# A fused hybrid-transformer kernel: query and key projections in another order, value products moved behind the first attention scores, and the meta keys of all heads handled once per query tile

## The chip, the cores and the metric

The kernel runs on one core of a Trainium2 chip. The metric is the device time of one execution in microseconds (us); lower is better.

## What is computed

Two transformer layers follow one another on a sequence of 512 tokens, with 16 meta tokens put in front (528 positions, width 1024). The change touches the first layer's latent attention (8 heads):

```python
q = (rmsnorm(c_q_raw, q_norm) @ w_uq).reshape(b, length, MLA_HEADS, MLA_NOPE + MLA_ROPE)
kv = (rmsnorm(c_kv_raw, kv_norm) @ w_ukv).reshape(b, length, MLA_HEADS, MLA_NOPE + MLA_V)
...
s = (jnp.einsum('bqhd,bkhd->bhqk', qn_b, k_nope)
     + jnp.einsum('bqhd,bkd->bhqk', qr_b, k_rope)).astype(jnp.float32) * scale
...
p = jax.nn.softmax(s, axis=-1).astype(v.dtype)
return jnp.einsum('bhqk,bkhd->bqhd', p, v)
```

The mask is causal. Beside it the first layer has a feed-forward block, a gated delta rule (a recurrence over chunks of 64) and another feed-forward block; the second layer has two more attentions. Everything is float32.

## The kernel before

The program is written out by hand, engine by engine: each engine has its own list of instructions, and counted semaphores order them. Nothing is scheduled by a tool, so the order in the code is the order on the engine, and a wait blocks everything behind it on that engine.

Most matrix products split both operands into a high and a low part (`WHI`, `WLO` of the weights, `CHI`, `CLO` of the latents) and do three fast products for one exact one (`mm3`, lines 562 to 564). Attention itself uses plain float32 products. The scratch memory for results, PSUM, has eight banks of 128 x 512 values; which bank is free decides much of the order. `PS[:, b, ...]` is bank b.

In the stretch that the change touches (about 498 to 604 us of the profiled execution) TensorE does, in order:

- **Queries**: eight tiles `t` of the query projection. Tiles 4 to 7 hold the rotary parts and go to banks 0 to 3, from where VectorE reads them (`ROT`, lines 1921 to 1927). Then it sums squares of the delta rule's queries and keys (`GSQ`, line 690, banks 4 and 5), and does tiles 2, 3, 0 and 1 (banks 6, 7, 4, 5). ScalarE takes logarithms of the sums (line 1333), switches its table to exp (line 1335), and copies the four query tiles (`QH`, line 1340).
- **Keys**: tiles 0, 1, 3, 2, two banks each, copied by ScalarE (`KH`, line 1345).
- **Values**: five tiles in the order meta tokens, then four blocks of 128 tokens (lines 716 to 718), copied by VectorE (`VM`, lines 1934 and 1937).
- **Attention** (`latent_attention`, once on each engine): 16 steps, in `LATENT`. A step is one tile of 128 queries for two heads (p = 0 and 1); the last query tile comes first. Steps 0 to 3 see 528 keys, more than a bank holds, so each head takes two banks and the next step's scores must wait until exp has read them (`WIDE` is 4). Later steps see 400, 272 and 144 keys and alternate between two pairs of banks.

In turn i TensorE does the scores of step i (line 774), transposes the probabilities of step i - 2 (line 785: the blocks of 128 keys; line 792: the 16 meta keys), and multiplies values by the probabilities of step i - 3 (line 808 for the blocks, line 813 for the meta keys). After the last step of a query tile it also spreads the softmax factors (line 824). `per_token` (lines 729 and 732) is a small piece of the delta rule done in turn 1. VectorE takes the row minima (lines 1949 and 1954; scores are negated), ScalarE the exponentials with their sums (`PB`, line 1365). ScalarE copies head 0's transposed blocks (`PTS`, line 1356) and the meta keys' ones of both heads (`PTM`, line 1358); VectorE copies head 1's (line 1968). In turns 6 to 13 VectorE also works on a convolution of the delta rule (`value_taps`, lines 1806 and 1809). GpSimd prepares exponents for the delta rule (lines 534 to 543) that ScalarE needs in turn 13 (`EU`, line 1381) and turn 17 (`IT`, line 1386).

Of the kernel before, what the change touches and what calls it, by code (L numbers as in the profile page):

```python
# [17 lines left out]
P = 128  # L18
# [3 lines left out]
T1 = N_META + SEQ  # L22
# [45 lines left out]
for _name, _c in [("ident", 128), ("ones", 128), ("bones", 128), ("cos", T1), ("sin", T1),  # L68
                  ("mA", 256), ("mB", 256), ("cneg", 4 * NCMP), ("c01", 4 * NCMP), ("i64", CH),
                  ("mlater", CH), ("hs", 4 * NH), ("lvl", LEVELS * CH), ("sel", 4 * 128),  # L70
                  ("oh", 383)]:
    TABS[_name] = _n
    _n += _c
# [4 lines left out]
def build(nc, io):  # L78
# [44 lines left out]
    def region(start, *items):  # L123
# [32 lines left out]
    VM, PB1, PTS1, PTM, DSB1, OTF1, NM1, RS1, RI1, NMF1, a_at1 = region(  # L156
        a_qk, ("VM", [P, 5, SEQ], f32), ("PB1", [P, 2, 2, T1], f32), ("PTS1", [P, 2, 2, SEQ], f32),
        ("PTM", [N_META, 2, 2, P], f32), ("DSB1", [P, SEQ], f32), ("OTF1", [P, SEQ], f32),
        ("NM1", [P, 4 * NH], f32), ("RS1", [P, 4 * NH], f32), ("RI1", [P, 4 * NH], f32),
        ("NMF1", [P, 4 * NH], f32))  # L160

# [109 lines left out]
    def halves(ap):  # L271
# [58 lines left out]
    vm_rdy, fm_rdy, row_st, kx_ld, qx_ld, px_d = (sem(x) for x in (  # L330
        "value_tile_copied", "latent_far_min_ready", "gate_rows_stored", "k_rows_spread",
# [114 lines left out]
    WIDE = sum(x["n"] > SEQ for x in LATENT)  # L446

# [109 lines left out]
    def _(pe):  # L557
# [124 lines left out]
        for t in (4, 5, 6, 7, 2, 3, 0, 1):  # L682
            if t == 2:

                pe.wait_ge(evac, START["uq"])
                pe.wait_ge(l_sq, 8)
                for b, (a, m) in enumerate(spans(0, T1)):
                    for g in range(4):
                        for i in range(2):
                            last = mm(PS[32 + 32 * i:40 + 32 * i, 4 + b, 0:m], tab("hs", NH * g, NH * (g + 1)),  # L690
                                      GSQ[:, 4 * i + g, a:a + m], start=g == 0, stop=g == 3)
                last.then_inc(l_ss, 1)
            elif t == 0:
                pe.wait_ge(l_r, 2)
# [3 lines left out]
            last.then_inc(uq_ps, 1)  # L698
        pe.wait_ge(uq_ps, 8)
        pe.sem_inc(mm_done, 1)  # L700

        pe.wait_ge(lo_rdy, START["ukv"] + 2)
        for t in (0, 1, 3, 2):
            if t == 0:
                pe.wait_ge(rot_rdy, 1)
            elif t >= 2:
                pe.wait_ge(q_act, 4 if t == 3 else 8)
            for b, (a, m) in enumerate(spans(0, T1)):
# [47 lines left out]
        def latent_attention():  # L756
            n = len(LATENT)
            for i in range(n + 3):
                if i < n:
                    x, s = LATENT[i], i % 2  # L760
                    if i == 0:
                        pe.wait_ge(vm_rdy, 4)
                    elif i == WIDE:
# [11 lines left out]
                    last.then_inc(s_ps, 1)  # L775
                if i == 1:
                    per_token()
                if 0 <= i - 2 < n:
                    x, s = LATENT[i - 2], i % 2
                    for p in range(2):  # L780
                        pe.wait_ge(exp_rdy, 2 * (i - 2) + p + 1)
                        if i >= 3:
# [1811 lines left out]
```

## Time and profile before

| | us |
|---|---|
| Median of 3 runs | 1636.67 |
| Lowest and highest run | 1636.23, 1639.49 |
| The profiled execution, its own time | 1633.94 |
| Its span, first to last instruction | 1632.3 |
| TensorE busy | 1574.4 (96%) |
| VectorE busy | 922.6 (57%) |
| ScalarE busy | 577.4 (35%) |
| GpSimd busy | 43.7 (3%) |
| Mean granted TensorE clock | 0.988 of full |

Busy shares are averages over stages with different limits. The granted clock is the share of TensorE's full speed that the chip allowed; it has two levels here, 1.0 (2.4 GHz) and 0.5 (1.2 GHz).

### The profile page before, as it was taken

To read this page: it belongs to the slowest core of one execution; us is meant where nothing else is said; L and a number is where in the kernel's file an instruction comes from. 1 tells how busy PE (TensorE), PEld (TensorE's weight loads), DVE (VectorE), ACT (ScalarE), POOL (GpSimd) and SP (SyncE) were. 2 spreads that over 40 slices of the span, in tenths; PEclk is the share of its full clock that TensorE was granted. 3 is DMA by queue.
4 is the path that set the end of the run, shared out by engine and by line. 5 is a ranking of instruction groups with operands and counts; after the bars stand their busy time and mean duration, and the time that the engine had idled before them with its cause. 6 is when DMAs were issued, how large, how long until landed. Compare 5 with 4: busy or idle time off the path is not lost.

```text
span 1632.3 us, 30415 instructions
## 1 busy us (share of the span) xinstructions
PE 1574.4 (96%) x12739; PEld 1366.1 (84%) x12739; DVE 922.6 (57%) x1408; ACT 577.4 (35%) x854; POOL 43.7 (3%) x41
## 2 busy tenths in 40 slices
PE   6999999999998998989999999999999899999998
PEld 6999999999996678877888888888888687775777
DVE  6655245556487478655444645533555643557872
ACT  5222122223255371224223322222222243556750
POOL 0000000000000600000000000000000000000000
PEclk9999999999999799999999999999999999999999
DMA  6443333332217300001323222232222433120002
GB/s 258 152 144 99 105 128 130 132 98 106 98 60 129 71 2 29 4 3 54 114 81 113 103 98 83 78 114 104 103 87 89 146 148 130 52 68 24 2 2 77
DMA packets 27476, 147.68 MB, mean 90 GB/s; under 512 B 2816, under 2 KB 3088, under 8 KB 16752
## 3 DMA queue, kind: packets, MB, share of 16 engines
q1 hardware_dynamic: 21616, 122.46, 21.7%
q0 software_dynamic: 5232, 22.68, 4.9%
q8 instruction: 78, 1.28, 0.3%
q10 hardware_dynamic: 528, 1.08, 0.2%
q14 instruction: 22, 0.18, 0.0%
HBM read 140.94 MB, written 5.27 MB: 90 GB/s over the span
## 4 chain that ended last, share of the span: by engine, by line
PE 88%; DVE 7%; issue 2%; ACT 2%; DMA 0%; DVEq 0%; SPq 0%; ACTq 0%
PE PS L562 24%; PE PS L563 24%; PE PS L564 24%; PE PS L842 2%; PE PS L852 2%; PE PS L877 2%; PE PS L774 2%; PE PS L864 1%; DVE UMB L2107 1%; DVE TTT L2139 1%; DVE WLO L1623 1%; PE PS L921 1%; PE PS L1147 1%; PE PS L937 1%; PE PS L785 1%
## 5 line engine op out<-in xcount | busy, mean ns | idle before, releaser
L562 PE MATMUL PS<-UH,WHI 128*128 128x264 f32 (+1 forms) x1120 | 337.2, 301 | 14.8 <-DVE UL L1633 11.1
L563 PE MATMUL PS<-UH,WLO 128*128 128x264 f32 (+1 forms) x1120 | 335.6, 300 | 0.0
L564 PE MATMUL PS<-UL,WHI 128*128 128x264 f32 (+1 forms) x1120 | 335.2, 299 | 0.0
L1194 ACT ACTIVATE WHI<-RAW 128x2048 fp32r<-128x2048 f32 (+3 forms) x124 | 210.3, 1696 | 293.6 <-PE PS L564 286.8
L1623 DVE TENSOR_TENSOR WLO<-RAW,WHI 128x2048 fp32r<-128x2048 f32 (+3 forms) x124 | 251.2, 2026 | 80.7 <-ACT WHI L1194 80.1
L562 PEld LDWEIGHTS PS<-UH,WHI 128*128 128x128 f32 x1120 | 211.8, 189 | 21.9 <-DVE WLO L1731 11.1
L563 PEld LDWEIGHTS PS<-UH,WLO 128*128 128x128 f32 x1120 | 211.8, 189 | 6.4 <-issue 0.2
L564 PEld LDWEIGHTS PS<-UL,WHI 128*128 128x128 f32 x1120 | 211.4, 189 | 6.3
L562 PE MATMUL PS<-UHS,WHI 128*128 128x512 f32 x520 | 205.2, 395 | 0.0
L564 PE MATMUL PS<-ULS,WHI 128*128 128x512 f32 x520 | 202.6, 390 | 0.0
L563 PE MATMUL PS<-UHS,WLO 128*128 128x512 f32 x520 | 202.5, 389 | 0.0
L1238 ACT ACTIVATE TANH<-SILU 128x528 f32<-128x528 f32 (+1 forms) x44 | 28.1, 639 | 258.3 <-DVE SILU L1683 258.3
L562 PEld LDWEIGHTS PS<-UHS,WHI 128*128 128x128 f32 x520 | 97.7, 188 | 22.1 <-issue 2.2
L563 PEld LDWEIGHTS PS<-UHS,WLO 128*128 128x128 f32 x520 | 97.7, 188 | 20.9 <-issue 1.0
L564 PEld LDWEIGHTS PS<-ULS,WHI 128*128 128x128 f32 x520 | 97.6, 188 | 20.2
L563 PE MATMUL PS<-GH,WLO 128*128 128x264 f32 x352 | 100.6, 286 | 0.0
L564 PE MATMUL PS<-GL,WHI 128*128 128x264 f32 x352 | 100.3, 285 | 0.0
L562 PE MATMUL PS<-GH,WHI 128*128 128x264 f32 x352 | 99.6, 283 | 0.0
L1683 DVE TENSOR_TENSOR SILU<-PS,RSTD 128x528 f32<-128x528 f32 (+1 forms) x44 | 30.8, 700 | 106.9 <-PE PS L564 104.4
L1708 DVE SCALAR_TENSOR_TENSOR H<-PS,H 128x528 f32<-128x528 f32 (+3 forms) x32 | 22.3, 698 | 112.5 <-PE PS L564 112.5
L562 PE MATMUL PS<-GHS,WHI 128*128 128x512 f32 x176 | 68.7, 390 | 0.0
L563 PE MATMUL PS<-GHS,WLO 128*128 128x512 f32 x176 | 68.5, 389 | 0.0
(403 smaller groups left out, 2703.5 us busy)
## 6 DMA issues: line engine op xcount, KB each, us to landing
RAW<-in_f2u SPq DMA_DIRECT2D x22, 1024.0 KB, 4.8
RAW<-in_f1u SPq DMA_DIRECT2D x21, 1024.0 KB, 4.8
ADA<-in_ada POOLq DMA_DIRECT2D x24, 512.0 KB, 4.5
RAW<-in_f1d SPq DMA_DIRECT2D x16, 704.0 KB, 4.1
RAW<-in_f2d SPq DMA_DIRECT2D x16, 704.0 KB, 4.1
RAW<-in_wi SPq DMA_DIRECT2D x10, 1024.0 KB, 4.8
RAW<-in_w SPq DMA_DIRECT2D x8, 1024.0 KB, 4.8
RAW<-in_mg SPq DMA_DIRECT2D x8, 1024.0 KB, 4.8
```

The source lines that it names most:

```text
L562: mm(out, WHI[:, slot, c:c + w], hi, start=first, stop=False)
L563: mm(out, WLO[:, slot, c:c + w], hi, start=False, stop=False)
L564: return mm(out, WHI[:, slot, c:c + w], lo, start=False, stop=last)
L774: last = mm(scores(i, p, k0, k1), q, KH[0:96, h, k0:k1], start=True, stop=True)
L842: last = mm(PS[:, 2 - 2 * s + p, c:c + m], P2[rows, q, P * x["qi"]:P * (x["qi"] + 1)], P2[rows, 10 + x["b"], a:a + m], start=True, stop=True)
L852: last = nc.tensor.transpose(PS[:, 4 + p, t * P:(t + 1) * P], PB2[:, s, p, t * P:(t + 1) * P], IDENT)
L877: last = mm(PS[rows, 6, P * x["j"]:P * (x["j"] + 1)], v, PTS2[:, s, p, t * P:(t + 1) * P], start=t == 0, stop=t == tiles_ - 1)
L1194: A(WHI[:, slot, 0:w], RAW[:, slot, 0:w], ACT.Copy).then_inc(hi_rdy, 1)
L1238: A(TANH[:, slot, 0:w], SILU[:, slot, 0:w], ACT.Tanh, scale=0.5).then_inc(tanh_rdy, 1)
L1623: TT(WLO[:, slot, 0:w], RAW[:, slot, 0:w], WHI[:, slot, 0:w].bitcast(f32), ALU.subtract).then_inc(lo_rdy, 1)
L1683: TT(SILU[:, slot, 0:w], psum(4 * slot, w), RSTD[:, c0:c0 + w], ALU.mult).then_inc(gn_rdy, 1)
L1708: STT(h, psum(4 * slot, w), 0.25, h, ALU.mult, ALU.add)\
```

## The change

- **Queries**: tiles 2 and 3 come before the sums of squares, tiles 0 and 1 after the keys' tiles 1, 0 and 3.
- **Keys**: tiles 1 and 0 are copied by VectorE, ahead of its `gate_exponents`; tiles 3 and 2 by ScalarE. ScalarE copies query tiles 2 and 3 before the logarithms.
- **Values**: two tiles before the first scores, two behind the scores of step 0, the meta tokens' behind those of step 1. VectorE copies each where its turn allows.
- **Minima**: in the four wide steps each head has its own semaphore count, reduction and minimum, so that head 0's exp does not wait for head 1's scores.
- **Meta keys**: VectorE copies each step's 16 meta probabilities of both heads into `PM` (128 x 2 x 8 heads x 16). Once per query tile TensorE transposes all 128 at once and multiplies them by a value tile in which the meta values stand once for each head, masked (`hm`), four products of full width. Since products of all heads now add to bank 6 over four steps, each query tile begins with a product of zeros that clears the bank. Per step, the two small transposes (line 792), the four records of small products (line 813) and ScalarE's `PTM` copy go.

```diff
+    def scored(i, p):
+
+        return 2 * i + p + 1 if i < WIDE else WIDE + i + 1
...
-        for t in (4, 5, 6, 7, 2, 3, 0, 1):
-            if t == 2:
-
-                pe.wait_ge(evac, START["uq"])
-                pe.wait_ge(l_sq, 8)
...
+        def up_query(t):
+
             for k in range(2):
                 last = mm3(PS[:, (t + 4) % 8, 0:SEQ], 0, (2 * t + k) * P, CHI[:, k, N_META:T1],
                            CLO[:, k, N_META:T1], k == 0, k == 1)
             last.then_inc(uq_ps, 1)
+
+        def up_key(t, b0):
+
+            for b, (a, m) in enumerate(spans(0, T1)):
+                last = mm3(PS[:, b0 + b, 0:m], 1, t * P, CHI[:, 2, a:a + m], CLO[:, 2, a:a + m], True, True)
+            last.then_inc(kn_ps, 1)
+
+        def up_value(t, b):
+
+            out = PS[:, b, 0:SEQ]
+
+            a = N_META + P * (t - 1)
+            hi, lo = (c[:, 2, a:a + P] for c in (CHI, CLO)) if t else (CHM[:, i, :] for i in range(2))
+            mm(out, hi, WHI[:, 1, SEQ:2 * SEQ], start=True, stop=False)
+            mm(out, lo, WHI[:, 1, SEQ:2 * SEQ], start=False, stop=False)
+            mm(out, hi, WLO[:, 1, SEQ:2 * SEQ], start=False, stop=True).then_inc(kn_ps, 1)
+
+        for t in (4, 5, 6, 7):
+            up_query(t)
+        pe.wait_ge(evac, START["uq"])
+        for t in (2, 3):
+            up_query(t)
+        pe.wait_ge(l_sq, 8)
+        for b, (a, m) in enumerate(spans(0, T1)):
+            for g in range(4):
+                for i in range(2):
+                    last = mm(PS[32 + 32 * i:40 + 32 * i, 4 + b, 0:m], tab("hs", NH * g, NH * (g + 1)),
+                              GSQ[:, 4 * i + g, a:a + m], start=g == 0, stop=g == 3)
+        last.then_inc(l_ss, 1)
+        pe.wait_ge(lo_rdy, START["ukv"] + 2)
+        pe.wait_ge(rot_rdy, 1)
+        up_key(1, 2)
+        up_key(0, 0)
+        pe.wait_ge(q_act, 4)
+        up_key(3, 6)
+        pe.wait_ge(l_r, 2)
+        for t in (0, 1):
+            up_query(t)
+        pe.wait_ge(kv_rdy, 2)
+        up_key(2, 2)
         pe.wait_ge(uq_ps, 8)
         pe.sem_inc(mm_done, 1)
-
-        pe.wait_ge(lo_rdy, START["ukv"] + 2)
-        for t in (0, 1, 3, 2):
-            if t == 0:
-                pe.wait_ge(rot_rdy, 1)
-            elif t >= 2:
-                pe.wait_ge(q_act, 4 if t == 3 else 8)
-            for b, (a, m) in enumerate(spans(0, T1)):
-                last = mm3(PS[:, 2 * t + b, 0:m], 1, t * P, CHI[:, 2, a:a + m], CLO[:, 2, a:a + m],
-                           True, True)
-            last.then_inc(kn_ps, 1)
-        for t in range(5):
-            if t % 2 == 0:
-                pe.wait_ge(k_act, t + 2)
-            a = 0 if t == 0 else N_META + P * (t - 1)
-            mm(PS[:, (0, 1, 2, 3, 6)[t], 0:SEQ], CHI[:, 2, a:a + P], WHI[:, 1, SEQ:2 * SEQ], start=True, stop=False)
-            mm(PS[:, (0, 1, 2, 3, 6)[t], 0:SEQ], CLO[:, 2, a:a + P], WHI[:, 1, SEQ:2 * SEQ], start=False, stop=False)
-            mm(PS[:, (0, 1, 2, 3, 6)[t], 0:SEQ], CHI[:, 2, a:a + P], WLO[:, 1, SEQ:2 * SEQ], start=False, stop=True)\
-                .then_inc(kn_ps, 1)
-        pe.wait_ge(kn_ps, 9)
-        pe.sem_inc(mm_done, 1)
+        pe.wait_ge(q_act, 8)
+        for t in (1, 2):
+            up_value(t, 3 + t)
...
+                        if i < WIDE or p:
+                            last.then_inc(s_ps, 1)
+                if i == 0:
+
+                    pe.wait_ge(k_act, 2)
+                    for t in (3, 4):
+                        up_value(t, 3 + t)
                 if i == 1:
+
+                    pe.wait_ge(kv_rdy, 6)
+                    up_value(0, 4)
+                    pe.wait_ge(kv_rdy, 8)
                     per_token()
+                    pe.wait_ge(kn_ps, 9)
+                    pe.sem_inc(mm_done, 1)
...
-                        if p == 0:
-                            last.then_inc(pt_ps, 1)
-                    if x["g"]:
-                        pe.wait_ge(den_rdy, x["g"])
-                    for p in range(2):
-                        last = nc.tensor.transpose(PS[0:N_META, 7, P * p:P * (p + 1)], PB1[:, s, p, 0:N_META], IDENT)
-                    last.then_inc(pt_ps, 1)
+                        last.then_inc(pt_ps, 1)
+                        if p == 0 and x["last"]:
+
+                            pe.wait_ge(pc_rdy1, i - 2)
+                            if x["g"]:
+                                pe.wait_ge(den_rdy, x["g"])
+                            nc.tensor.transpose(PS[:, 7, 0:P], PM[:, x["g"] % 2, :, :].rearrange("q h m -> q (h m)"),
+                                                IDENT)
...
+                    if x["j"] == 0:
+
+                        mm(PS[:, 6, :], ZERO[:, :], ZERO[:, :].unsqueeze(1).to_broadcast([P, 4, P]), start=True,
+                           stop=False)
                     for t in range(x["qi"] + 1):
                         for p in range(2):
                             h = x["j"] + 4 * p
-                            mm(PS[CH * p:CH * (p + 1), 6, P * x["j"]:P * (x["j"] + 1)],
-                               VM[:, 1 + t, CH * h:CH * (h + 1)], PTS1[:, s, p, t * P:(t + 1) * P],
-                               start=t == 0, stop=False)
-                    for p in range(2):
-                        h = x["j"] + 4 * p
-                        last = mm(PS[CH * p:CH * (p + 1), 6, P * x["j"]:P * (x["j"] + 1)],
-                                  VM[0:N_META, 0, CH * h:CH * (h + 1)], PTM[:, s, p, :], start=False, stop=True)
+                            last = mm(PS[CH * p:CH * (p + 1), 6, P * x["j"]:P * (x["j"] + 1)],
+                                      VM[:, 1 + t, CH * h:CH * (h + 1)], PTS1[:, s, p, t * P:(t + 1) * P],
+                                      start=False, stop=False)
+                    if x["last"]:
+                        for j in range(4):
+                            last = mm(PS[:, 6, P * j:P * (j + 1)], VM[:, 0, P * j:P * (j + 1)], PTM[:, :],
+                                      start=False, stop=j == 3)
...
+        def copy_query(i, t):
+
+            act.wait_ge(uq_ps, 4 + i + 1)
+            for p in range(2):
+                A(QH[0:CH, 2 * t + p, :], PS[CH * p:CH * (p + 1), 4 + t, 0:SEQ], ACT.Copy,
+                  scale=scale).then_inc(q_act, 1)
+
+        def copy_key(i, t, b):
+
+            act.wait_ge(kn_ps, i)
+            for p in range(2):
+                A(halves(KH[0:CH, 2 * t + p, :]), PS[CH * p:CH * (p + 1), b:b + 2, 0:HT], ACT.Copy).then_inc(k_act, 1)
+
+        copy_query(0, 2)
+        copy_query(1, 3)
+        chain(A(CST[:, 3:4], EPS_AP, ACT.Ln))
         act.wait_ge(gt_d, 4)
         act.wait_ge(l_ss, 1)
         for i, rows in enumerate((R8, A8)):
             A(RW[R8, i, PAD:].rearrange("p (b n) -> p b n", b=2), PS[rows, 4:6, 0:HT], ACT.Ln,
               bias=CST[rows, 4 + i:5 + i], scale=64.0 if i == 0 else 1.0).then_inc(l_r, 1)
         chain(A(CST[:, 3:4], EPS_AP, ACT.Exp))
-        scale = -float(96) ** -0.5
-        for i, t in enumerate((2, 3, 0, 1)):
-            act.wait_ge(uq_ps, 4 + i + 1)
-            for p in range(2):
-                A(QH[0:CH, 2 * t + p, :], PS[CH * p:CH * (p + 1), 4 + t, 0:SEQ], ACT.Copy,
-                  scale=scale).then_inc(q_act, 1)
-        for i, t in enumerate((0, 1, 3, 2)):
-            act.wait_ge(kn_ps, i + 1)
-            for p in range(2):
-                A(halves(KH[0:CH, 2 * t + p, :]), PS[CH * p:CH * (p + 1), 2 * t:2 * t + 2, 0:HT],
-                  ACT.Copy).then_inc(k_act, 1)
+        copy_key(3, 3, 6)
+        copy_query(2, 0)
+        copy_query(3, 1)
+        copy_key(4, 2, 2)
...
-                    A(PTS1[:, s, 0, 0:w], PS[:, 4, 0:w], ACT.Copy)
+                    last = A(PTS1[:, s, 0, 0:w], PS[:, 4, 0:w], ACT.Copy)
                     act.wait_ge(pt_ps, 2 * (i - 2) + 2)
-                    A(PTM[:, s, :, :], PS[0:N_META, 7, 0:2 * P].rearrange("m (p q) -> m p q", p=2), ACT.Copy)\
-                        .then_inc(pt_rdy, 1)
+                    if LATENT[i - 2]["last"]:
+                        last = A(PTM[:, :], PS[:, 7, 0:P], ACT.Copy)
+                    last.then_inc(pt_rdy, 1)
...
+        for i, t in enumerate((1, 0)):
+            dve.wait_ge(kn_ps, i + 1)
+            for p in range(2):
+                V.tensor_copy(halves(KH[0:CH, 2 * t + p, :]), PS[CH * p:CH * (p + 1), 2 * t:2 * t + 2, 0:HT])\
+                    .then_inc(kv_rdy, 1)
         gate_exponents()
...
+        for i, c in enumerate((CHI, CLO)):
+            last = V.tensor_copy(CHM[:, i, :].rearrange("k (r m) -> k r m", r=NH),
+                                 c[:, 2, 0:N_META].bitcast(f32).unsqueeze(1).to_broadcast([P, NH, N_META]))
+        last.then_inc(kv_rdy, 1)
+
+        def value_tile(t):
+
+            if t:
+                dve.wait_ge(kn_ps, 4 + t)
+                V.tensor_copy(VM[:, t, :], PS[:, 3 + t, 0:SEQ]).then_inc(kv_rdy, 1)
+            else:
+                dve.wait_ge(kn_ps, 9)
+                TT(VM[:, 0, :].rearrange("r (j p d) -> r p j d", j=4, p=2),
+                   PS[:, 4, 0:SEQ].rearrange("r (p j d) -> r p j d", p=2, j=4),
+                   tab("hm", 0, NH).rearrange("r (p j) -> r p j", p=2).unsqueeze(3).to_broadcast([P, 2, 4, CH]),
+                   ALU.mult).then_inc(kv_rdy, 1)
...
+                    if i < WIDE:
+                        for p in range(2):
+                            c = 2 * i + p
+                            dve.wait_ge(s_ps, scored(i, p))
+                            V.tensor_reduce(NMF1[:, c:c + 1], scores(i, p, 0, w - P), AX.X, ALU.min).then_inc(far_rdy, 1)
+                            minima(p)
...
+                    dve.wait_ge(exp_rdy, 2 * i)
+                    V.tensor_copy(PM[:, x["g"] % 2, x["j"]:NH:4, :], PB1[:, (i - 1) % 2, :, 0:N_META])
...
+                    value_tile(4)
+                    value_tile(0)
+                    TS(ZERO[:, :], IDENT, 0.0, None, ALU.mult)
+                    dve.wait_ge(kv_rdy, 10)
+                    dve.sem_inc(evac, 1)
```

What this does to the order on the engines is shown at three places. ScalarE first, from the rotary keys' copies (`KH<-PR`) to the first exponentials (`PB`), before:

```order
L1328 ACTIVATE KH<-PR 32x528 x8
L1291 ACTIVATE GSQ<-PRC 128x1056
L1333 ACT_TABLE_LOAD
L1333 ACTIVATE RW<-PS,CST 8x528 x2
L1335 ACT_TABLE_LOAD
L1335 ACTIVATE CST<-CST 128x1
L1340 ACTIVATE QH<-PS 64x512 x8
L1345 ACTIVATE KH<-PS 64x528 x8
```

And of the change:

```order
L1361 ACTIVATE KH<-PR 32x528 x8
L1324 ACTIVATE GSQ<-PRC 128x1056
L1369 ACTIVATE QH<-PS 64x512 x4
L1380 ACT_TABLE_LOAD
L1380 ACTIVATE CST<-CST 128x1
L1384 ACTIVATE RW<-PS,CST 8x528 x2
L1386 ACT_TABLE_LOAD
L1386 ACTIVATE CST<-CST 128x1
L1376 ACTIVATE KH<-PS 64x528 x2
L1369 ACTIVATE QH<-PS 64x512 x4
L1376 ACTIVATE KH<-PS 64x528 x2
```

Four query copies and a table load now stand ahead of the logarithms (`RW`), and four key copies are gone from ScalarE. VectorE in the same place, of the change (before, the four `gate_exponents` rows, `RW` and `TR`, followed the `QH` additions directly, then five `VM` copies):

```order
L1972 TENSOR_TENSOR QH<-ROT 32x512 x8
L1977 COPY KH<-PS 64x528 x4
L1897 SCALAR_TENSOR_TENSOR RW<-RW 8x576
L1898 TENSOR_TENSOR TR<-RW,TR 8x576
L1901 SCALAR_TENSOR_TENSOR RW<-RW,TR 8x576
L1902 SCALAR_TENSOR_TENSOR RW<-RW 8x576
L1984 CAST CHM<-CHI 128x128
L1984 CAST CHM<-CLO 128x128
L1992 COPY VM<-PS 128x512
L2019 TENSOR_REDUCE NMF_104<-PS 128x1
L2012 ISA PS,NM_101<-PS,TAB,NMF_104 128x128
```

One value copy is left ahead of the first minimum, with four key copies and two small casts in the place of the others. Last, TensorE around the first scores (lines 706 to 708 are value products, 787 scores, 744 and 747 `per_token`), of the change:

```order
L787 MATMUL PS<-KH,QH 128x512 [waits key_or_value_copied,k_nope_copied,k_rope_ready]
...
L706 MATMUL PS<-WHI,CHI 128x512 [waits k_nope_copied]
...
L787 MATMUL PS<-KH,QH 128x512 [waits exp_ready]
...
L706 MATMUL PS<-WHI,CHM 128x512 [waits key_or_value_copied]
...
L744 MATMUL PS<-TAB,RW 128x24 [waits gate_vector_steps,key_or_value_copied]
...
L787 MATMUL PS<-KH,QH 128x512 [waits k_tile_in_psum,exp_ready]
```

Before, the first of these rows was preceded by all five value tiles and followed directly by the scores of step 1.

## Rows read from the trace of the kernel before

**Rows 1.** Windows: busy us (and count) per engine, granted clock, DMA share, GB/s.

```profile
core 0: us, PE busy (x) PEld busy (x) DVE busy (x) ACT busy (x) POOL busy (x), PEclk, DMA share, GB/s
498.00:526.50 28.50, 24.43 (x134) 17.73 (x133) 22.31 (x30) 20.47 (x32) 1.55 (x2) 1.00 0.88 151
526.50:531.20 4.70, 2.33 (x9) 1.28 (x9) 2.03 (x6) 0.86 (x3) 0.00 (x0) 0.99 0.98 117
531.20:555.80 24.60, 23.46 (x83) 15.72 (x83) 7.91 (x24) 6.73 (x18) 12.47 (x3) 0.52 0.62 115
566.50:592.10 25.60, 25.60 (x246) 18.80 (x246) 24.04 (x70) 17.48 (x56) 2.21 (x1) 1.00 0.01 2
```

**Rows 2.** Timeline of TensorE (PE), wide steps: start, duration, line, operands, count, [idle before].

```profile
526.51 2.31 PE L774 MATMUL PS<-KH,QH 96*128 96x512 f32 x8 [0.39 <-DVE VM L1937]
531.18 4.45 PE L774 MATMUL PS<-KH,QH 96*128 96x512 f32 x8 [2.36 <-ACT PB L1365]
535.47 2.22 PE L729 MATMUL PS<-TAB,RW 128*128 128x24 f32 x10
537.62 1.87 PE L732 MATMUL PS<-RW,TAB 8*128 8x9 f32 x8
```

**Rows 3.** Timeline of VectorE (DVE) and ScalarE (ACT), step 0.

```profile
528.86 0.99 DVE L1949 TENSOR_REDUCE NMF<-PS 128x2 f32<-128x800 f32 x1 [2.01 <-PE PS L774]
529.88 0.36 DVE L1954 CUSTOM_DVE_ANT_0 PS<-PS,TAB,NMF 128x128 f32<-128x128 f32 x1
530.34 0.70 ACT L1365 ACTIVATE PB<-PS,NM 128x528 f32<-128x528 f32 x1 [4.26 <-DVE NM L1954]
```

**Rows 4.** Timeline of TensorE, projections.

```profile
508.01 3.73 PE L690 MATMUL PS<-GSQ,TAB 128*8 128x264 f32 x32 [2.41 <-ACT GSQ L1291]
522.34 0.51 PE L716 MATMUL PS<-WHI,CHI 128*128 128x512 f32 x1 [0.27 <-ACT KH L1345]
...
525.73 0.39 PE L718 MATMUL PS<-WLO,CHI 128*128 128x512 f32 x1
```

**Rows 5.** Timeline of ScalarE, projections.

```profile
506.79 1.08 ACT L1291 ACTIVATE GSQ<-PRC 128x1056 f32<-128x1056 f32 x1 [1.47 <-DVE PRC L1816]
511.83 1.28 ACT L1333 ACT_TABLE_LOAD   x1 [3.96 <-PE PS L690]
513.13 1.41 ACT L1333 ACTIVATE RW<-PS,CST 8x528 f32<-8x528 f32 x2
...
516.09 4.93 ACT L1340 ACTIVATE QH<-PS 64x512 f32<-64x512 f32 x8
521.04 5.03 ACT L1345 ACTIVATE KH<-PS 64x528 f32<-64x528 f32 x8
```

**Rows 6.** Timeline of VectorE, projections.

```profile
509.41 5.56 DVE L1927 TENSOR_TENSOR QH<-ROT 32x512 f32<-32x512 f32 x8
...
517.36 0.75 DVE L1857 SCALAR_TENSOR_TENSOR RW<-RW 8x576 f32<-8x576 f32 x1
...
524.06 2.79 DVE L1937 COPY VM<-PS 128x512 f32<-128x512 f32 x4
```

**Rows 7.** Chain that ended last, turn 4 (start, length, engine, line, count).

```profile
555.81 1.54 PE PS L774 x4
557.35 0.88 PE PS L785 x8
558.23 0.22 PE PS L792 x2
558.44 1.02 PE PS L808 x16
559.47 0.36 PE PS L813 x4
```

**Rows 8.** Timeline of GpSimd (POOL), and of ScalarE where it reads IX.

```profile
543.15 4.04 POOL L534 TENSOR_TENSOR EU<-EU,GPA 128x2304 f32<-128x2304 f32 x1 [41.16 <-DMA EU<-rows]
563.63 5.08 POOL L543 TENSOR_TENSOR IX<-IX,TAB 128x2304 f32<-128x2304 f32 x1
...
602.40 2.57 ACT L1386 ACTIVATE IT<-IX 128x384 f32<-128x384 f32 x6
```

**Rows 9.** Windows: a place in the second layer's attention.

```profile
1475.00:1480.00 5.00, 5.00 (x35) 3.60 (x34) 1.54 (x11) 2.12 (x10) 0.00 (x0) 0.50 0.02 3
```

More of the change, by code:

```diff
@@ L329, in build @@
     sink_s, se_rdy = sem("sink_shifted"), sem("state_decayed")
-    vm_rdy, fm_rdy, row_st, kx_ld, qx_ld, px_d = (sem(x) for x in (
-        "value_tile_copied", "latent_far_min_ready", "gate_rows_stored", "k_rows_spread",
+    kv_rdy, row_st, kx_ld, qx_ld, px_d = (sem(x) for x in (
+        "key_or_value_copied", "gate_rows_stored", "k_rows_spread",
         "q_rows_spread", "exponents_shifted"))
@@ L681, in _ @@
         pe.wait_ge(c_lo, 1)
-        for t in (4, 5, 6, 7, 2, 3, 0, 1):
-            if t == 2:
-                pe.wait_ge(evac, START["uq"])
-                pe.wait_ge(l_sq, 8)
-                for b, (a, m) in enumerate(spans(0, T1)):
[L688 to L694, printed above, removed]
+        def up_query(t):
             for k in range(2):
@@ L881, in _ @@
         pe.wait_ge(kr_rdy, NH)
[L882 removed]
+        pe.wait_ge(k_act, 4)
+        pe.wait_ge(kv_rdy, 4)
         latent_attention()
@@ L1932, in _ @@
         dve.wait_ge(kr_rdy, NH)
-        dve.wait_ge(kn_ps, 5)
-        V.tensor_copy(VM[0:N_META, 0, :], PS[0:N_META, 0, 0:SEQ]).then_inc(vm_rdy, 1)
-        for t in range(1, 5):
-            dve.wait_ge(kn_ps, 5 + t)
-            V.tensor_copy(VM[:, t, :], PS[:, (0, 1, 2, 3, 6)[t], 0:SEQ]).then_inc(vm_rdy, 1)
-        dve.wait_ge(vm_rdy, 5)
-        dve.sem_inc(evac, 1)
+        for i, c in enumerate((CHI, CLO)):
[6 more added lines that the diff above has]
+                V.tensor_copy(VM[:, t, :], PS[:, 3 + t, 0:SEQ]).then_inc(kv_rdy, 1)
+            else:
+                dve.wait_ge(kn_ps, 9)
[3 more added lines that the diff above has]
+                   ALU.mult).then_inc(kv_rdy, 1)
         def latent_attention():
             n = len(LATENT)
+            value_tile(1)
             for i in range(n + 6):
@@ L1946, in latent_attention, with minima @@
                     w = x["n"]
-                    both = PS[:, 0:4:2, 0:w - P] if w > SEQ else PS[:, 2 * s:2 * s + 2, 0:w - P]
-                    dve.wait_ge(s_ps, i + 1)
-                    V.tensor_reduce(NMF1[:, 2 * i:2 * i + 2], both, AX.X, ALU.min).then_inc(fm_rdy, 1)
-                    dve.wait_ge(fm_rdy, i + 1)
-                    for p in range(2):
+                    def minima(p):
                         c = 2 * i + p
                         z = scores(i, p, w - P, w)
+                        dve.wait_ge(far_rdy, scored(i, p))
                         V.tensor_tensor_reduce(z, z, tab("mB", P, 2 * P), 1.0, NMF1[:, c:c + 1], ALU.add, ALU.min,
                                                NM1[:, c:c + 1]).then_inc(max_rdy, 1)
+                    if i < WIDE:
[4 more added lines that the diff above has]
+                            minima(p)
+                    else:
+                        dve.wait_ge(s_ps, scored(i, 1))
+                        V.tensor_reduce(NMF1[:, 2 * i:2 * i + 2], PS[:, 2 * s:2 * s + 2, 0:w - P], AX.X, ALU.min)\
+                            .then_inc(far_rdy, 1)
+                        for p in range(2):
+                            minima(p)
+                if i == 0:
+                    value_tile(2)
+                    value_tile(3)
+                if 0 <= i - 1 < n:
+                    x = LATENT[i - 1]
+                    dve.wait_ge(exp_rdy, 2 * i)
+                    V.tensor_copy(PM[:, x["g"] % 2, x["j"]:NH:4, :], PB1[:, (i - 1) % 2, :, 0:N_META])
                 if 0 <= i - 1 < n and LATENT[i - 1]["last"]:
```

24 lines of the change are left out of this document (11 added, 13 removed).

## The prediction, made before the changed kernel had run

> **What bounds the kernel now.** I read the busy shares first: TensorE is busy 96% of the span, so a gain must come from its instructions, its waits or its clock. Then the windows by stage [rows 1]. The stretch that the change touches has three kinds of time. From 498 to 526.5 us projections run, with waits. In the next 29.3 us, to 555.8, stand the four wide steps of attention; there the granted clock is 0.99 at first and 0.52 (nearly always the lower level) from 531.2 on. From 566.5 to 592.1 TensorE reads as fully busy at full clock, but VectorE is busy 24.04 of 25.60 us: both are near their bound.
>
> The timeline of TensorE shows the wide steps [rows 2]: eight records of scores take 2.31 us, then TensorE waits 2.36 us, then the clock has fallen and the same eight records take 4.45 us. What ends that wait is exp: the minimum over both heads' far keys (0.99 us) needs both heads' scores, and the exp of head 0 (0.70 us) comes after it [rows 3]. The next scores need the same banks. So a wait of one chain costs twice: itself, and the clock behind it.
>
> **The change, part by part.** I follow the new order from the last unchanged work to step 4, with durations of rows, and compare the start of step 4's scores (555.81 before [rows 7]).
>
> *Projections.* Query tiles 2 and 3 (12 fast products) now fill the 2.41 us that TensorE waits for `GSQ` [rows 4]. A fast product of 512 columns costs 0.24 us: 15 value products begin between 522.34 and 525.73 [rows 4], 3.39 us for 14. The sums of squares then start about 508.2, 0.2 later than before, and end at 511.9. ScalarE meanwhile copies four query halves after `GSQ` (ends 507.9; 0.62 each, 4.93 for 8 [rows 5]) to 510.4 and loads the log table (1.28) by 511.9, behind the sums of squares. Before, that load began only at 511.83 [rows 5]. So the logarithms (1.41) run 512.0 to 513.4, exp's table to 515.0, and then eight copies of 0.62 (two key, four query, two key) end at 520.0. Before, ScalarE's sixteen copies ended at 526.07 (521.04 + 5.03). On VectorE, the `QH` additions end at 514.97 [rows 6]; four key copies follow, priced as the value copies of the same kind, 0.70 (2.79 for 4 [rows 6]), to 517.8, four gate steps of 0.78 (0.75 for one [rows 6]) to 520.9, two small casts (0.25 each, an estimate from the 128-column operation of 0.36 [rows 3]) and one value copy to 522.1. TensorE does 18 key products of 264 columns (about half of 0.24 each) to 514.15, by when the logarithms are done, 12 query products to 517.0, six more key products to 517.7, waits for the query copies until 518.8 and does two value tiles (6 x 0.24) to 520.25. First scores: 520.3 instead of 526.51. **Saved: 6.2.**
>
> *Wide steps.* Head by head, the scores take 1.15 us, the far minimum 0.53 (half of 0.99 and a little), the masked one 0.45 with its read, exp 0.70 and 0.1 of signalling: about 1.8 from scores to exp's end.
> - Step 0: scores 520.3 to 522.6. Two value tiles behind them, to 524.05. VectorE comes free at 522.1, so the exps end at 523.95 and 524.95.
> - Step 1: scores 524.1 to 526.4, no wait; meta values to 527.1; `per_token`. That took from 535.47 to 539.49 at half clock (537.62 + 1.87 [rows 2]); its price at full clock lies between half (2.0) and all (4.0). The scores in the same rows went from 4.45 to 2.31 with the clock, so I take half: to 529.1.
> - Step 2: its exps of step 1 are ready at 528.5, so scores 529.1 to 531.35, transposes of step 0 (0.88 [rows 7]) to 532.25. VectorE has two more value tiles, the clearing zeros and the gate columns in its way and reaches step 2's minimum at 530.95; exp of head 0 ends at 533.3. TensorE waits 1.15.
> - Step 3: scores 533.4 to 535.7, transposes to 536.6, a clearing product (0.24) and value products of step 0 (1.02 [rows 7]) to 537.85.
>
> Step 4 starts at 537.85: 17.5 us for what took 29.3. **Saved: 11.8.** Of it the clock is the larger half: three blocks of scores at 4.45 instead of 2.31 alone are 6.4.
>
> *Meta keys.* Per step TensorE saves 0.22 and 0.36 us [rows 7], 2.3 per query tile. New per query tile are a transpose (0.11), the clearing product (0.24) and four products of full width. No row shows those: they cost at least 0.13 each (16 records for 8 half-width pairs, 1.02 [rows 7]) and at most 0.25 (400 columns cost 0.77, from 1.54 for two heads [rows 7], times 128/400). I take the upper end, 1.0 for four. Net 0.9 less per query tile, 3.8 in all. But VectorE gains a copy per step (0.15, estimated from the same small operation), and from 566.5 to 592.1 it has only 1.56 us to spare [rows 1], against eight copies of 0.15. So in turns 6 to 13 I count nothing. Turns 4 and 5 lie before that: 1.1 saved. At the tail ScalarE sheds three `PTM` copies (0.3 each beyond its overlap) and TensorE's last group of meta products gives about 0.6 back. **Saved: 1.0 together.**
>
> *Costed at nothing.* The gate steps end at 520.9 instead of 518.1, so the gate rows are stored, spread and subtracted later on GpSimd. That chain runs from 543.15 to 568.71 and is read at 602.40 [rows 8]. With both moves (2.8 later, reader 19 earlier) 12 us are left; were the cover gone, each microsecond late would be one on the path. Value tiles now copied in turns 0 and 1 are not needed before turn 3. Weight loads wait for none of this.
>
> **Sum**: 6.2 + 11.8 + 1.0 = 19.0. Against the profiled execution, 1633.94, that is 1614.9; the median of the runs is 2.7 above it, so the same sum gives **1617.7**.
>
> **What the skill says, weighed.** TensorE was idle 2.36 us, and the granted clock behind it was the lower level, 0.52 over 24.6 us [rows 1, 2]. The Trainium skill, TensorE: Matmul & The Clock Gate, section "Why this matters for your kernels", warns of idle gaps longer than this one. By that rule the 2.36 us is not what brought the clock down, and filling it need not keep it up. The row says that it fell right there; I follow the row.
>
> **Rivals.**
> - *The clock falls all the same* (28 in 100). Step 3 still waits 1.15 us, with transposes ahead of it. Against: 2.41 us of waiting before `GSQ` brought no fall, the windows from 498 to 526.5 read 1.00 [rows 1, 4]. For: in the second layer's attention the clock is 0.50 though no wait is seen in those 5 us [rows 9], so work of the same kind does run at the lower level. If it falls before step 3, the scores cost 2.1 more and transposes, values and the next steps some 5; if in step 1, three blocks of scores (6.4), `per_token` (1.9) and the rest about 12. Middle 9: 1626.7. The page's rule above ends here too.
> - *VectorE and the coupling of engines eat the rest* (12 in 100). PE and DVE are so evenly loaded in turns 6 to 13 that the four wide products and the extra copies add where I count nothing: up to 4 x 1.0 and 8 x 0.3, less what TensorE sheds there: 3 us, 1621.
> - *Nothing comes through* (3 in 100): a stall behind moves up and takes all. The only late chain is GpSimd's, and it would need 31 us more, so little speaks for it: 1636.
> - *Slower* (3 in 100): the clock falls in the first scores and stays low to the end of the attention. New first scores to step 4 would cost up to 16 more, and the 46.6 us behind (555.81 to 602.40 [rows 7, 8]) as much again: about 40 over my sum, 1660. It turns into a loss once matmul work of more than 19 us runs at half clock; before, the level was back by 555.8 [rows 1], after only 24.6 us, so I give it little.
>
> **How the numbers follow.** My forecast holds 54 in 100, its own range 1613 to 1622 (`per_token` at full price +1.9, wide products at 0.13 each -1.9, the engines' signalling over eight wide scores +-1.5). The range for 8 in 10 reaches over the second rival and most of the first: **1612 to 1629**. About 0.2% (3.3 us) is what a measurement can tell from no change. Faster 0.94, same 0.03, slower 0.03.
>
> **What would show it.** The profile of the change should have the first scores about 520.3; granted clock 1.00 from there to 538; scores of step 4 at about 538; VectorE near 95% busy in the 25 us of turns 6 to 13 and that stretch as long as before; GpSimd's chain done by about 572. I am wrong if the clock reads 0.5 for more than a few microseconds there, if the first scores come after 522, or if turns 6 to 13 take over 27 us.

## The result, and the profile after

The kernel became **slower**: 1658.45 us (median of four runs, 1654.38 to 1659.21) against 1638.08 for the kernel before beside it, ratio 1.0128, 95% interval 1.011 to 1.0145. Forecast were 1617.7 us and 94 in 100 for faster. The profiled executions are 1659.21 us (span 1657.6) and 1633.94 (span 1632.3): 25.3 us apart. The mean granted clock over the span hardly differs (0.987 and 0.988).

I read the windows of the changed kernel first, over the stretch that the change touches, and one place of the second layer's feed-forward, which it does not touch. Against [rows 1]:

```profile
core 0: us, PE busy (x) PEld busy (x) DVE busy (x) ACT busy (x) POOL busy (x), PEclk, DMA share, GB/s
535.00:545.00 10.00, 9.12 (x32) 6.21 (x32) 4.80 (x16) 3.28 (x8) 0.00 (x0) 0.50 0.70 138
545.00:550.00 5.00, 5.00 (x46) 3.63 (x44) 2.55 (x7) 2.69 (x9) 3.06 (x1) 1.00 1.05 217
550.00:562.00 12.00, 10.30 (x86) 7.29 (x85) 11.93 (x18) 5.12 (x17) 11.74 (x4) 1.00 0.07 15
562.00:573.50 11.50, 0.40 (x3) 0.16 (x2) 11.40 (x3) 0.27 (x1) 10.42 (x2) 0.65 0.00 0
573.50:580.00 6.50, 6.46 (x36) 4.63 (x36) 5.29 (x18) 3.06 (x9) 0.00 (x0) 0.57 0.01 3
1130.00:1170.00 40.00, 40.00 (x173) 32.15 (x172) 19.42 (x19) 9.21 (x9) 0.00 (x0) 1.00 0.23 80
```

Three things are to be seen. The clock fell after all, from about 535 to 545 us. From 562 to 573.5 TensorE does next to nothing (0.40 us), while VectorE reads as busy 11.40 us with three instructions; behind that, to 580, the clock reads 0.57. And in the last line TensorE starts 173 matmuls in 40 us at full clock; the same window of the kernel before has 178:

```profile
1130.00:1170.00 40.00, 40.00 (x178) 33.15 (x177) 20.32 (x21) 11.00 (x11) 0.00 (x0) 1.00 0.29 98
```

When I set the two traces instruction against instruction, the loss is spread out. VectorE's last addition out of PSUM before the projections (into `PRC`) starts at 499.81 us before and at 503.58 after: 3.8 us lost in code that is the same. From the end of the attention to the end of the program it is 21.5 more (the last multiplication into `OTF`, which I take as the end of the attention from here on, starts at 602.61 before and at 606.36 after, 3.75 later; the end comes 25.3 later). So the attention itself came out at nothing.

The timeline of TensorE in the wide steps of the changed kernel, which answers to [rows 2]:

```profile
523.96 2.23 PE L787 MATMUL PS<-KH,QH 96*128 96x512 f32 x8
...
527.77 2.33 PE L787 MATMUL PS<-KH,QH 96*128 96x512 f32 x8
...
530.73 1.20 PE L744 MATMUL PS<-TAB,RW 128*128 128x24 f32 x10
531.86 1.05 PE L747 MATMUL PS<-RW,TAB 8*128 8x9 f32 x8
532.84 2.61 PE L787 MATMUL PS<-KH,QH 96*128 96x512 f32 x8
535.29 1.95 PE L812 MATMUL PS<-TAB,PB 128*128 128x128 f32 x8
538.12 4.45 PE L787 MATMUL PS<-KH,QH 96*128 96x512 f32 x8 [0.88 <-ACT PB L1410]
...
545.85 1.61 PE L787 MATMUL PS<-KH,QH 96*128 96x400 f32 x4
```

The waits are gone but for 0.88 us, and step 4 starts at 545.85 instead of 555.81. Then comes what the forecast did not have. GpSimd's chain, which answers to [rows 8], and the long instructions of VectorE in the same stretch:

```profile
546.94 4.04 POOL L539 TENSOR_TENSOR EU<-EU,GPA 128x2304 f32<-128x2304 f32 x1 [41.16 <-DMA EU<-rows]
551.08 6.03 POOL L541 TENSOR_SCALAR EU<-EU 128x2304 f32<-128x2304 f32 x1
557.18 4.05 POOL L544 TENSOR_TENSOR IX<-QX,GPA 128x2304 f32<-128x2304 f32 x1
561.32 6.02 POOL L546 TENSOR_SCALAR IX<-IX 128x2304 f32<-128x2304 f32 x1
567.42 5.09 POOL L548 TENSOR_TENSOR IX<-IX,TAB 128x2304 f32<-128x2304 f32 x1
```

```profile
543.49 0.18 DVE L2034 COPY PM<-PB 128x32 f32<-128x32 f32 x1
...
548.81 2.21 DVE L2034 COPY PM<-PB 128x32 f32<-128x32 f32 x1
...
552.90 4.25 DVE L2034 COPY PM<-PB 128x32 f32<-128x32 f32 x1
...
558.50 2.77 DVE L2034 COPY PM<-PB 128x32 f32<-128x32 f32 x1
...
561.65 11.14 DVE L1851 TENSOR_SCALAR TAB<-PRC,COL 128x528 f32<-128x528 f32 x2
...
586.16 0.90 DVE L1851 TENSOR_SCALAR TAB<-PRC,COL 128x528 f32<-128x528 f32 x2
```

A copy of 32 columns takes 0.18 us at 543.49 and 4.25 at 552.90. It ends at 557.15, as GpSimd's second instruction does (551.08 + 6.03 = 557.11); the others end at 551.02 and 561.27, at the ends of the first and third (550.98 and 561.23), and the two taps that took 11.14 us end at 572.79, just behind the end of the fifth (572.51). VectorE's work out of PSUM between them (0.71, 0.36, 0.55 us) keeps its length. So these instructions stood still: 2.03 + 4.07 + 2.59 + 10.24 = 18.9 us.

### The profile page after: what moved, and what is told of

It reads as the page before. It is cut to its first block, busy times and chain, and to the rows that moved or that the text cites. A ratio compares the mean times of both kernels' runs of the same rounds, so it can differ in the third digit from the quotient of the medians.

```text
span 1657.6 us, 30330 instructions
## 1 busy us (share of the span) xinstructions
PE 1590.7 (96%) x12683; PEld 1366.3 (82%) x12683; DVE 945.9 (57%) x1435; ACT 571.0 (34%) x839; POOL 43.8 (3%) x41
## 4 chain that ended last, share of the span: by engine, by line
PE 87%; DVE 9%; issue 2%; ACT 1%; DMA 0%; DVEq 0%; SPq 0%; ACTq 0%
PE PS L567 24%; PE PS L568 24%; PE PS L569 24%; PE PS L874 2%; PE PS L884 2%; PE PS L909 2%; PE PS L787 1%; PE PS L896 1%; DVE UMB L2191 1%; DVE TTT L2223 1%; DVE WLO L1668 1%; DVE TAB L1851 1%; PE PS L954 1%; PE PS L1180 1%; PE PS L970 1%
## 5 line engine op out<-in xcount | busy, mean ns | idle before, releaser
L567 PE MATMUL PS<-UHS,WHI 128*128 128x512 f32 x520 | 208.6, 401 | 0.0
L569 PE MATMUL PS<-ULS,WHI 128*128 128x512 f32 x520 | 206.0, 396 | 0.0
L568 PE MATMUL PS<-UHS,WLO 128*128 128x512 f32 x520 | 205.9, 396 | 0.0
L569 PE MATMUL PS<-GLS,WHI 128*128 128x512 f32 x176 | 69.5, 395 | 0.0
```

The source lines that it names most:

```text
L567: mm(out, WHI[:, slot, c:c + w], hi, start=first, stop=False)
L568: mm(out, WLO[:, slot, c:c + w], hi, start=False, stop=False)
L569: return mm(out, WHI[:, slot, c:c + w], lo, start=False, stop=last)
```

## The experiments

Two theories were set up. **A, placement**: the new table `hm` (8 columns, 32 bytes in a partition) lies ahead of the arena, which holds nearly every buffer but the weights, so the arena moved from byte 100736 of the partition, a multiple of 64 and of 128, to 100768, a multiple of 32 only; TensorE reads its operands slower there. The rival, **B**, is that the loss comes with the change's own work. **C, standing**: VectorE's accesses from SBUF to SBUF stand while a GpSimd instruction runs; the earlier attention brought the two together. Its rival, **D**, is that these long instructions wait for another engine or are made by the profile. The Trainium skill, SBUF — State Buffer, section "Who interferes with whom", states C's rule: VectorE's copies and scalings in a mode that uses two ports, and its operations with two SBUF inputs (against a GpSimd instruction that reads SBUF), need ports that GpSimd uses too, and whichever comes later blocks until the other's instruction is done; reductions never do. The trace's ends above agree with it.

**Where the arena starts.** In both kernels one line was edited:

```diff
-    arena = top[0]
+    arena = top[0] + 32     # b32; b64: + 64 (kernel before), a32: + 32 (changed kernel)
```

> The kernel before with one edit: the arena that holds the operands of the dense products (and nearly everything else) starts 32 bytes later in each partition, at the address that it has in the changed kernel, a multiple of 32 and no longer of 64. No instruction changes. Theory A (placement: the changed kernel loses its time outside the touched stretch because its new 8-column table moved the arena by 32 bytes): 1656 to 1664 us, ratio about 1.013, with the 128x512 weight products near 401 ns instead of 395 and the 128x264 ones near 303 instead of 301. Rival B (the loss comes with the change's own work, by the clock or the order of instructions): 1638 us, within 0.2%.

> The kernel before with the arena 64 bytes later, again a multiple of 64. Theory A, if the multiple counts: 1638 us, as before. Theory A in the form that any move of the arena costs (a distance to another buffer, not a multiple): 1656 to 1664. Rival B: 1638.

> The changed kernel with its arena 32 bytes further on, a multiple of 64 again; its instructions stay. Theory A: the 3.8 us ahead of the projections and the 21.5 us behind the attention are back, and what is left is the attention stretch, where the trace showed gain and loss about equal: 1634 to 1640 us. Rival B: 1655 to 1660, as the changed kernel.

Measured: `b32` 1662.8 us, ratio 1.0152 (1.0127 to 1.0176): the kernel before, with no instruction changed, lost 25 us by the ratio. `b64` 1641.9, 1.0031 (1.0018 to 1.0045). `a32`, the changed kernel at a multiple of 64, 1640.2, 1.0024 (1.0009 to 1.0039). A stands for the loss outside the attention, and B falls. But both kernels at a multiple of 64 that is none of 128 are a little above the kernel before, and above what was expected of `b64` (1638).

**Which operand.** The next two kernels are `b64` with only some buffers 32 bytes off (in `b64_w` the small tables between weights and arena also move, by 64 bytes):

```diff
-    UH, UL, a_u = region(arena, ...)             # b64_uh
-    UHS, ULS, a_v = region(arena, ...)
-    a_v += 1024
+    UH, UL, a_u = region(arena - 32, ...)
+    UHS, ULS, a_v = region(arena - 32, ...)
+    a_u, a_v = a_u + 32, a_v + 1024 + 32
```

```diff
+    top[0] += 32                                 # b64_w
     WHI_AT = top[0]
...
+    top[0] += 32
     TAB = place("TAB", [P, NTAB])
```

> The kernel before with its arena 64 bytes later (measured 1641.9 us, 1.003), and in it only the four tiles UH, UL, UHS and ULS, the moving operands of most dense products, start 32 bytes off the multiple of 64. Everything else stays. If the loss of the changed kernel is TensorE's reading of a moving operand that is off the multiple of 64: 1655 to 1662 us, since these tiles feed about three quarters of the dense products. If it is another engine's access or another tile's: 1642.

> The kernel before with its arena 64 bytes later and only the weights' buffers WHI and WLO 32 bytes off the multiple of 64. If an operand off that multiple costs wherever TensorE reads it, the weight loads too: 1655 or more. If only the moving operand counts, since the weight loads run under the products before: 1640 to 1644, as with the arena alone.

Measured: `b64_uh` 1654.9, 1.0122 (1.0108 to 1.0137), at the lower end of what was expected if the moving operands count; `b64_w` 1660.4, 1.0153 (1.014 to 1.0167). Of the two cases set out for `b64_w` the first holds: weight buffers off by 32 bytes cost as much as everything in the arena off by 32 bytes. One number sorts the kernels, the matmuls that start in the 40 us from 1130 to 1170, where the moving operands are `UHS` and `ULS` and the clock is 1.00 in all:

| kernel | moving operands | weights | matmuls in 40 us | ratio |
|---|---|---|---|---|
| before | multiple of 128 | multiple of 128 | 178 | 1 |
| `b64` | 64 | 128 | 176 | 1.0031 |
| changed | 32 | 128 | 173 | 1.0128 |
| `b32` | 32 | 128 | 173 | 1.0152 |
| `b64_uh` | 32 | 128 | 173 | 1.0122 |
| `b64_w` | 64 | 32 | 173 | 1.0153 |
| `a224` (below) | 128 | 128 | 179 | 0.9989 |

(The figures are the largest power of two, up to 128 bytes, that divides the start.) One of the two operands off the multiple of 64 is enough. Each trace of the two holds a check of this: from 890 to 930 us the moving operands are nearly all `MH` and `ML`, which `b64_uh` leaves where they are in `b64`, and there it has 176 matmuls like `b64`, while `b64_w` has 173.

**The arena at a multiple of 128, and GpSimd's chain cut.** `a224` is the changed kernel with `arena = top[0] + 224`, and all that follow are edits of it. In `a224_short` two of GpSimd's instructions are gone, so that its exponents lack the running sum of the gates; it is there for its time alone:

```diff
-        G2(EU[:, :, :], EU[:, :, :], along(GPA[:, 0, :], NU), ALU.subtract).then_inc(px_d, 1)
-        pool.wait_ge(px_d, 1)
+        pool.sem_inc(px_d, 1)
...
-        G2(IX[:, :, :], QX[:, :, :], along(GPA[:, 0, :], NU), ALU.subtract).then_inc(px_d, 1)
-        pool.wait_ge(px_d, 3)
-        G1(IX[:, :, :], IX[:, :, :], 16.0, None, ALU.min).then_inc(px_d, 1)
+        G1(IX[:, :, :], QX[:, :, :], 16.0, None, ALU.min).then_inc(px_d, 2)
```

> The changed kernel with its arena 224 bytes further on: like the arena of the kernel before it starts 128 bytes past a multiple of 256. The kernels with arenas 64 past a multiple of 128 both came out 0.2 to 0.3% over the kernel before. If that is the placement once more (Theory A, second part: 64 bytes off the line of 128 costs a little as well): 1633 to 1637 us, within 0.1% of the kernel before. If it is not, and a multiple of 64 is all that counts: 1640 again.

> As the one with its arena 224 bytes further on, with GpSimd's chain cut from five instructions to three: the two subtractions are left out, 8.1 us of 25.5 (the exponents EU and IX lack the running sum of the gates, so the outputs differ). VectorE and ScalarE keep every instruction. Theory C (VectorE stands while GpSimd holds what they share): the chain ends 8.1 us earlier, VectorE waits less by about that, and the attention ends 6 to 9 us earlier than with the full chain. Rival D (VectorE's long instructions wait for another engine or are the profile's making): no change of the time, and the long ones stay long.

Measured: `a224` 1634.8, ratio 0.9989 (0.9978 to 1.000), as the second part of A has it. In it the placement's loss is gone and the attention's outcome is bare: wide steps that start step 4 at 539.23 us, and an end of the attention (last `OTF`) at 600.80, only 1.8 us before that of the kernel before. `a224_short`: 1627.7, 0.9936 (0.992 to 0.9953); its attention ends at 595.61, 5.2 us earlier, a little under what C expected and not what D did. The chain ends at 561.2 (571.1 in `a224`), and the first taps, 5.67 us long, end there as well:

```profile
544.28 5.47 DVE L2031 COPY PM<-PB 128x32 f32<-128x32 f32 x1
...
551.12 4.73 DVE L2031 COPY PM<-PB 128x32 f32<-128x32 f32 x1
555.32 0.55 DVE L2049 COPY PTS<-PS 128x384 f32<-128x384 f32 x1
555.78 5.67 DVE L1848 TENSOR_SCALAR TAB<-PRC,COL 128x528 f32<-128x528 f32 x2
```

**Keeping VectorE clear of the chain, in two ways.** The copy into `PM` was written as a reduction over an axis of one element (`a224_red`), the value taps were started six turns later (`a224_taps`), both were done (`a224_both`, and `a32_both` on the arena of `a32`), and the taps alone were moved in the kernel before (`b_taps`).

```diff
-                    V.tensor_copy(PM[:, x["g"] % 2, x["j"]:NH:4, :], PB1[:, (i - 1) % 2, :, 0:N_META])
+                    V.tensor_reduce(PM[:, x["g"] % 2, x["j"]:NH:4, :],
+                                    PB1[:, (i - 1) % 2, :, 0:N_META].unsqueeze(3), AX.X, ALU.min)
...
-            for t0, i0 in ((8, 6), (10, 10)):
+            for t0, i0 in ((8, 12), (10, 16)):
```

> The changed kernel with its arena at a multiple of 64, and VectorE kept clear of GpSimd's five long instructions: the copy of the meta keys' probabilities into PM is written as a reduction over an axis of one element (same engine, same elements, another operation), and the taps of the value channels start at turns 12 and 16 instead of 6 and 10. Theory C (VectorE's copies, scalings and taps stand still while a GpSimd instruction holds something that they share; about 18.8 us of waiting in the trace): the attention ends 12 to 18 us earlier than in the kernel before, 1619 to 1627 us, with PM's writes at about 0.2 us each. Rival D (those long instructions of VectorE are only what the profile makes of a wait for another engine): 1634 to 1640, like the kernel with the arena alone put right.

> Arena at 224, and of the two remedies only the first: the meta keys' probabilities are written into PM by a reduction over an axis of one element. Theory C: PM's writes fall from 3 to 4 us to about 0.2 each, but the first taps now meet the chain earlier and stand in its place, so that only 0 to 4 us are won of the 9 or more that PM's copies stood; if reductions stand as copies do, PM's writes stay at 2 to 4 us and nothing is won. Rival D: PM's writes stay long.

> The changed kernel with its arena at 224 (1634.8 us) and of the two remedies only the second, the value taps at turns 12 and 16; PM is still written by a copy. Theory C: PM's copies go on standing behind each of GpSimd's instructions, 2 to 4 us each and 10 to 16 us in all, so most of the gain is missing: 1629 to 1634. If PM's copies matter little: 1624.4, as with both.

> Arena at 224, PM by the reduction and the taps at turns 12 and 16. By Theory A's second part it is 3 to 4 us under its twin with the arena 32 bytes further on (1627.9): 1623 to 1625 us. By the first part alone 1628. The trace shall show what is left of the forecast of 18 us: clock at full in the wide steps, taps at 0.9 to 1.5 us a turn behind the chain.

> The kernel before, with only the value taps moved to turns 12 and 16. There the taps begin at 568.2 us as GpSimd's chain ends, and VectorE is the bound of the turns either way, so that moving its work by six turns changes nothing: 1634 to 1639. If the move of the taps by itself is what made the best version fast, this comes near 1625 too.

| kernel | us | ratio (95%) | attention ends |
|---|---|---|---|
| `a32_both` | 1627.9 | 0.9942 (0.9923 to 0.9961) | no usable trace |
| `a224_red` | 1632.1 | 0.9968 (0.9953 to 0.9982) | 597.47 |
| `a224_taps` | 1629.7 | 0.9961 (0.9946 to 0.9976) | 598.80 |
| `a224_both` | 1624.4 | 0.9912 (0.9893 to 0.9931) | 587.16 |
| `b_taps` | 1640.7 | 1.0023 (1.0006 to 1.0039) | 605.41 |

`a32_both` came out a microsecond above what C expected, `a224_taps` and `a224_both` within it. In the timeline of `a224_red` the same 32 columns, in the middle of the chain, take 0.18 us as a reduction, and the taps stand in their place:

```profile
549.81 0.18 DVE L2034 TENSOR_REDUCE PM<-PB 128x32 f32<-128x32 f32 x1
...
550.38 8.62 DVE L1851 TENSOR_SCALAR TAB<-PRC,COL 128x528 f32<-128x528 f32 x2
...
561.62 4.05 DVE L1854 SCALAR_TENSOR_TENSOR TAB<-PRC,COL,TAB 128x528 f32<-128x528 f32 x2
```

That decides between C and D: engine, operand, size and moment are the same, only the operation differs. It is also what that section of the Trainium skill says of reductions, and the trace's 0.18 us agrees. In `a224_taps` it is the other way round: five copies into `PM` take 1.98 to 4.25 us. (The clock read 0.50 in its profiled execution from 531.5 to 541.8, and step 4 came at 542.62, 3.4 us later than in `a224`, so its end of the attention understates what the late taps win.) Either remedy alone leaves most of the standing; both together end the attention 13.6 us before `a224`. The window 550 to 570 us of `a224` and of `a224_both`:

```profile
550.00:570.00 20.00, 11.91 (x78) 8.28 (x76) 19.78 (x19) 4.41 (x14) 19.75 (x4) 0.83 0.01 1
```

```profile
550.00:570.00 20.00, 20.00 (x184) 16.09 (x186) 14.57 (x51) 12.41 (x43) 19.12 (x4) 1.00 0.01 2
```

GpSimd is busy in both. TensorE does 184 matmuls instead of 78. `b_taps` shows that moving the taps is no gain by itself: it came out some 4 us slower by the ratio, a little above what was expected. Its trace doesn't put that on the taps: from the first scores to the end of the attention it takes 76.1 us (529.27 to 605.41), as the kernel before does (526.51 to 602.61). The 2.8 us between them were lost ahead of the first scores, where the clock read 0.58 from 488 to 492 us and 0.66 from 508 to 513, and 5.4 more behind the attention; why is open. The best version is therefore `a224_both`, 0.9% under the kernel before and 2% under the change as it was made.

## Why the prediction was wrong

**Projections: right.** Said was 520.3 for the first scores. The changed kernel has 523.96, starting 3.8 us late; `a224` has 520.39. Not all of these 3.8 us are placement: in the changed kernel's trace the clock reads 0.57 from 490 to 494, where the kernel before reads 1.00. `b32`, whose trace reads 1.00 there, is 1.8 us late at the same place (501.56), so I put about 2 us on placement and the rest on the clock.

**Wide steps: right in the order, half right on the clock.** The wait that I left before step 3 (1.15) measured 0.88, `per_token` at full clock 2.1 (2.0 taken). Step 4 was to start at 537.85. It starts at 539.23 in `a224`, where the clock read 0.50 from about 530.7 to 533.9, and at 539.00 in `a224_red`, where it stayed at 1.00 from 527 to 537 and which had started 1.3 us late (501.11 against 499.81): without that delay 537.7, as forecast. In the changed kernel itself the fall lasted from 535 to 545 and step 4 came at 545.85: 4.2 us of the 18.0 were missing, after taking off the 3.8 of the late start. So my first rival came true in part; its price was 9, and it measured 4.2 by the start of step 4. What made the clock fall in some executions and not in others is open: the instructions and their order are the same in `a224` and `a224_red` up to the operation on 32 columns, and `a224_taps`, the same up to this point, had it low for 10 us.

**Meta keys, turns 6 to 13: the step failed.** I priced the copy into `PM` at 0.15 us "from the same small operation" and it does take 0.18, when GpSimd is idle. I had left the fact that the copy reads and writes SBUF out of account. Three of them took 9.2 us in the changed kernel.

**"Costed at nothing": the step that failed most inside the attention.** I took GpSimd's chain as something that is waited for, found 12 us of slack, and stopped there. Its place hardly moved, since it waits for a transfer (543.15 before, 544.79 in `a224`), but step 4 of the attention came 16.6 us earlier (539.23 instead of 555.81), 18.2 against the chain. Before, the first taps began at 568.24 us, half a microsecond ahead of the chain's end (568.71), and took 1.17 us instead of 0.89: no room was left between chain and taps, and a gain ahead of them was bound to run VectorE into the chain. In `a224` the standing of copies and taps sums to 19.4 us, and the two gains of 18 that I forecast were given back there, shown by `a224_both`, which gets 13.6 us of them back at the end of the attention.

**The sum: a term that was left out.** The table's 32 bytes stand nowhere in it. I had read `hm` in the diff, and looked at it only as an operand of one multiplication. It cost about 23 us (from `a224` to the changed kernel: ratios 0.9989 and 1.0128, 1.4%), more than the whole gain that I forecast, and it decides the sign. The rival on the slower side was a clock that stays low to the end of the attention; that was not seen. Two sums of the prediction don't come out as written: the terms for the meta keys (1.1, three times 0.3, and 0.6) give 1.4 or 2.6 by the sign of the last, not 1.0, and those of the slower rival (16 and 46.6) more than 40. Neither changes the outcome.

Of the 19.0 us forecast, `a224_both` has 12.1 by the medians (1636.49 to 1624.39), 14.4 by the ratio. Its trace has 15.5 at the end of the attention (602.61 to 587.16), so most of what is missing was lost behind it, in code that is the same: 1029.7 us in the kernel before, 1031.2 in `a224`, 1036.8 in `a224_both`. There the clock of `a224_both` read 0.73 and 0.76 from 1280 to 1300 us and 0.66 from 1400 to 1410, where `a224` reads 1.00; by my estimate these lost 2.7, 2.4 and 3.4 us, and `a224` lost 1.7 of the kind (0.83 from 1300 to 1310). Whether the earlier end of the attention brings such falls, or only this execution had them, is open: the six runs of `a224_both` reach from 1617.97 us (mean granted clock 0.993) to 1627.48 (0.988).

## What to carry to other kernels

Look at what an edit does to addresses before looking at what it does to instructions: a small table placed ahead of the big buffers moves the start of every operand, and one line that puts the start back on a multiple of 128 bytes settled it here. And an engine that nobody waits for is still a partner in time: when a gain pulls work forward, list what it will now run beside, above all VectorE's copies, scalings and two-input operations from SBUF to SBUF beside long GpSimd instructions. A chain that ended just as the other began is a warning, not a reassurance.

## What the runs showed of the hardware that was not expected

- With the moving operands or the weights of dense 512-column products at a multiple of 32 but not of 64 bytes in the partition, TensorE started 173 matmuls in 40 us instead of 178, about 3% fewer, at the same granted clock (1.00); over the kernel that cost 1.2 to 1.5%. A multiple of 64 but not of 128 cost 0.2 to 0.3% (176 in 40 us). Whether it is the read of TensorE itself, or the writes of the other engines into those buffers beside it, the runs do not separate; that TensorE is busy all through the window and starts fewer speaks for the read.
- It hit the 512-column products more than the 264-column ones: the mean of `UHS` by `WHI` went from 395 to 401 ns and 205.2 to 208.6 us in all, that of `UH` by `WHI` at 264 columns only from 286 to 287. There the start of the buffer is not that of every operand: a slice of `UH` is cut into two halves of 1056 bytes, so in the kernel before every second half already starts 32 bytes off a multiple of 64, and moving the arena by 32 bytes makes the halves change places. From one start to the next the products of the first halves went from 120.2 to 122.0 ns in `b32`, and those of the second stayed at 121.3. No run tests this by itself.
- A VectorE copy of 32 columns took up to 5.47 us beside GpSimd, 30 times its own length; VectorE's reads of PSUM beside it were not touched, nor were a reduction (0.18) and a reciprocal (0.20) from SBUF to SBUF in `a224_both`, where a subtraction with two operands in SBUF (`OTL`) took 1.39 instead of 0.69. The chain of GpSimd took its usual length (25.6 us in the changed kernel and before) or up to 0.8 us more.
